# Splitting the down product's operands during the last tiles of the up product, without a fence between the two

## What is computed

```
def conv_ffn(a, buf, w_up, w_conv, b_conv, w_down):
    u = a @ w_up                                   # 1024 -> 2 x 2816
    full = jnp.concatenate([buf, u], axis=1)
    c = b_conv
    for j in range(CONV_W):                        # three taps over time
        c = c + w_conv[j] * full[:, j:j + t]
    gate, val = jnp.split(c, 2, axis=-1)
    y = (jax.nn.gelu(gate) * val) @ w_down         # 2816 -> 1024
    return y, full[:, t:]
```

## Time and profile before

| what | us |
|---|---|
| median of 3 runs | 1949.39 |
| lowest and highest run | 1946.25, 1952.33 |
| the profiled execution's own time | 1946.59 |
| its span, first to last instruction | 1944.8 |
| PE busy in the span | 1807.3 (93%) |
| DVE busy | 1125.4 (58%) |
| ACT busy | 726.3 (37%) |
| PE's part of the chain that ended last | 81% |
| mean granted TensorE clock | 0.959 |

### The profile page before, as it was taken

The page is one execution under the profiler, slowest core; times in us unless marked ns, Lnnn a source line. Parts: engine busy times, 40 slices in busy tenths (PEclk is TensorE's granted clock), DMA queues, the critical chain, the costliest instruction groups (busy, mean ns, idle before and its releaser), DMA issues.

```text
span 1944.8 us, 34321 instructions
## 1 busy us (share of the span) xinstructions
PE 1807.3 (93%) x13384; PEld 1617.6 (83%) x13384; DVE 1125.4 (58%) x2363; ACT 726.3 (37%) x1313; POOL 38.4 (2%) x65
## 2 busy tenths in 40 slices
PE   6899898989999979999999998887989999979997
PEld 5788456989999979988479995445989999979987
DVE  7974465568777652263334865666568777652264
ACT  5323345543233242254323332656543333242252
POOL 1400000000000000000000000000000000000000
PEclk9999788999999989999999996999999999989999
DMA  4133678212222132221031133773212222132211
GB/s 177 66 61 132 212 260 293 87 42 89 87 79 83 41 132 86 78 90 57 21 108 57 55 124 121 265 266 132 88 44 88 87 80 82 41 132 87 77 44 49
DMA packets 77948, 204.13 MB, mean 105 GB/s; under 512 B 12530, under 2 KB 14882, under 8 KB 77314
## 3 DMA queue, kind: packets, MB, share of 16 engines
q1 hardware_dynamic: 75762, 190.36, 29.3%
q0 software_dynamic: 2064, 12.06, 1.8%
HBM read 190.81 MB, written 10.40 MB: 103 GB/s over the span
## 4 chain that ended last, share of the span: by engine, by line
PE 81%; DVE 9%; SPq 3%; ACT 3%; issue 2%; DMA 1%; DVEq 0%; ACTq 0%
PE psum L412 42%; PE psum L585 12%; PE psum L2203 7%; PE psum L2159 4%; PE psum L420 2%; SPq L1312 2%; PE psum L844 1%; PE psum L2352 1%; PE psum L1354 1%; PE psum L507 1%; PE psum L1329 1%; PE psum L521 1%; DVE sb_arena_r L372 1%; DVE sb_ring_r L372 1%; SPq L1296 1%
## 5 line engine op out<-in xcount | busy, mean ns | idle before, releaser
L412 PE MATMUL psum<-sb_a_sb_r,sb_ring_r 128*128 128x288 f32 x1408 | 297.1, 295 | 0.0
L412 PE MATMUL psum<-sb_a_sb_r,sb_arena_r 128*128 128x288 f32 x1344 | 276.5, 296 | 0.0
L412 PE MATMUL psum<-sb_y_sb_r,sb_ring_r 128*128 128x288 f32 x960 | 262.6, 298 | 0.5 <-DVE sb_ring_r L372 0.5
L412 PEld LDWEIGHTS psum<-sb_a_sb_r,sb_ring_r 128*128 128x128 f32 x1408 | 230.9, 188 | 0.4
L412 PEld LDWEIGHTS psum<-sb_a_sb_r,sb_arena_r 128*128 128x128 f32 x1344 | 217.0, 188 | 0.0
L372 DVE TENSOR_TENSOR sb_ring_r<-sb_ring,sb_ring_r 128x1024 fp32r<-128x1024 f32 (+1 forms) x90 | 116.2, 1295 | 169.1 <-ACT sb_ring_r L369 168.1
L412 PE MATMUL psum<-sb_y_sb_r,sb_arena_r 128*128 128x288 f32 x704 | 207.1, 294 | 6.3 <-DVE sb_a_sb_r L372 6.2
L369 ACT ACTIVATE sb_ring_r<-sb_ring 128x1024 fp32r<-128x1024 f32 (+1 forms) x90 | 99.8, 1114 | 300.6 <-PE psum L412 249.3
L412 PEld LDWEIGHTS psum<-sb_y_sb_r,sb_ring_r 128*128 128x128 f32 x960 | 174.9, 189 | 1.6 <-DVE sb_ring_r L372 1.0
L585 PE MATMUL psum<-sb_arena_r 128*128 128x288 f32 x960 | 161.6, 303 | 8.2 <-DVE sb_arena_r L372 8.2
L412 PE MATMUL psum<-sb_arena_r,sb_ring_r 128*128 128x288 f32 x1056 | 146.0, 299 | 20.9 <-DVE sb_arena_r L372 20.9
(11 more groups left out here) (402 smaller groups left out, 3130.2 us busy)
## 6 DMA issues: line engine op xcount, KB each, us to landing
sb_ring<-w SPq DMA_DIRECT2D x166, 512.0 KB, 3.6
sb_ring<-wd SPq DMA_DIRECT2D x32, 704.0 KB, 4.1
sb_arena<-sb_v SPq DMA_DIRECT2D x64, 256.0 KB, 5.5
sb_arena<-moba_v SPq DMA_DIRECT2D x56, 256.0 KB, 6.4
sb_ring<-moba_k SPq DMA_DIRECT2D x32, 256.0 KB, 4.1
sb_a_sb<-moba_k SPq DMA_DIRECT2D x32, 256.0 KB, 5.6
sb_ring<-sb_k SPq DMA_DIRECT2D x32, 256.0 KB, 4.1
sb_a_sb<-sb_k SPq DMA_DIRECT2D x32, 256.0 KB, 5.5
```

The source lines that it names most:

```text
L412: ins = e.eng.matmul(out[:, half, :], fr(w[p][:, k, :]), fr(x[q][:, k, cols]), start=(first and k == 0 and i == 0), stop=(last and k == kb ...
```

## The change

The 22 high parts `ffh` no longer lie in one array. Each block has a place of its own (`ffh_at`): blocks 0 to 3 in free space behind `fo`, blocks 4 to 7 behind the `wx` slabs (where `plew` was), blocks 8 to 14 over the `wx` slabs, blocks 15 to 21 over the convolution's buffers and `fo`. `plew` moves to the place of the first buffers of the convolution. Blocks 0 to 7 thus have places that nothing else uses during the up product.

ACT and DVE split blocks 0 to 7 and down slab 0 between the steps of the last four up tiles. The fence is replaced by a bare `e.mark()` on each engine (the drain and the step on the stage semaphore, with no wait); behind it ACT and DVE go on with blocks 8 to 10 or 12 to 14, slab 1, and the rest. Block 15 and later wait on ACT for the last gated row, blocks 20 and 21 for the store of `fo`, as the last blocks did before. `pe_down` has the same matmuls in the same order, written out because the blocks are now single arrays. SP's queue and POOL's instructions keep their order.

```diff
@@ -1686,6 +1686,7 @@
             tiles(ROUNDS, 2 * REST)
             e.splits += 2 * FT
             acc.skip(2 * FT)
+            e.mark()
 
         def act_up(e, acc):
 
@@ -1702,10 +1703,15 @@
                 act.wait_ge(acc_ready, n0 + n - 3 + i * RING)
                 act_high(e, slabs[:, n % RAW], split[n % 4][0], wh_ready)
 
+            def high_parts(first, last):
+
+                for m in range(first, last):
+                    act.wait_ge(geg_ready, g0 + m + 1)
+                    act_high(e, ff[:, m, :], ffh[m], xh_ready)
+
             def pairs_of(i, count):
                 for j in range(count):
 
-                    pr = 4 * i + j
                     for v in range(2):
                         if not isinstance(i, int) or 8 * i + 2 * j + v + AHEAD < 2 * FT:
                             split_slab(i, 2 * j + v + AHEAD)
@@ -1720,6 +1726,13 @@
                         act.activation(u[:, 2 + TP:TU].rearrange("p (b t) -> p b t", b=NB)[:, :, 2:],
                                        psum[:, 2 * s + 1, TP - HALF:HALF].rearrange("p (b t) -> p b t", b=NB), ACT.Copy)\
                            .then_inc(copied["act"], 1)
+                        if isinstance(i, int) and i == ROUNDS:
+                            if j == 0:
+                                high_parts(3 + 3 * v, (6, 8)[v])
+                            elif v == 0:
+                                act_split_down(e, 0, (acc_ready, n0 + 2 * FT - 2))
+                            else:
+                                high_parts(8, 12)
 
                     act.wait_ge(conv_d, g0 + j + 1 + i * 4)
                     act.activation(cb[2 * (j % 2)], cb[2 * (j % 2)], ACT.Gelu_apprx_tanh).then_inc(conv_a, 1)
@@ -1727,7 +1740,16 @@
             pairs_of(0, 4)
             with act.Fori(1, ROUNDS) as i:
                 pairs_of(i, 4)
+            high_parts(0, 3)
             pairs_of(ROUNDS, REST)
+            e.mark()
+            act_split_down(e, 1, (acc_ready, n0 + 2 * FT))
+            high_parts(12, 15)
+            act.wait_ge(geg_ready, g0 + FT)
+            high_parts(15, 20)
+            act.wait_ge(stored, 16 * (6 if e.downs == 0 else 12))
+            high_parts(20, FT)
+            e.parts += FT
             e.raws = [x + 2 * FT // RAW for x in raws]
             acc.skip(2 * FT)
             e.ups += 1
@@ -1739,6 +1761,17 @@
             base = layer * NVEC
             w0 = e.splits - AHEAD
             v.wait_ge(fst_in, 16 * (layer + 1))
+
+            def low_parts(first, last):
+
+                for m in range(first, last):
+                    v.wait_ge(xh_ready, e.parts + m + 1)
+                    dve_low(e, ff[:, m, :], ffh[m], ff[:, m, :], xl_ready)
+
+            def low_down(n):
+
+                v.wait_ge(wh_ready, w0 + 2 * FT + n + 1)
+                dve_low(e, dslabs[:, n % DRING], *dsplit[n % 2], wl_ready)
 
             def pairs_of(i, count):
                 for j in range(count):
@@ -1769,9 +1802,17 @@
                         o = fo[:, bass.ds(m, 1), :].rearrange("p m x -> p (m x)")
                         v.tensor_copy(o[:, 0:2], u[:, TP:2 + TP])
                         e.st.do(v.tensor_copy(o[:, 2:18].rearrange("p (b j) -> p b j", j=2), us[:, :, TS:TS + 2]))
+                        if isinstance(i, int) and i == ROUNDS and w == 0:
+                            if j == 0:
+                                low_parts(0, 3)
+                            else:
+                                low_down(0)
+                                low_parts(6, 8)
                     v.wait_ge(conv_a, g0 + j + 1 + i * 4)
                     v.tensor_tensor(ff[:, bass.ds(4 * i + j, 1), :].rearrange("p m t -> p (m t)"), cb[2 * (j % 2)],
                                     cb[2 * (j % 2) + 1], ALU.mult).then_inc(geg_ready, 1)
+                    if isinstance(i, int) and i == ROUNDS and j == 0:
+                        low_parts(3, 6)
 
             for u in ub:
                 e.st.do(v.memset(u[:, 0:2], 0.0))
@@ -1780,7 +1821,12 @@
                 pairs_of(i, 4)
                 e.st.leave(ROUNDS)
             pairs_of(ROUNDS, REST)
-            e.splits = w0 + 2 * FT
+            e.mark()
+            low_parts(8, 11)
+            low_down(1)
+            low_parts(11, FT)
+            e.parts += FT
+            e.splits = w0 + 2 * FT + 2
             acc.skip(2 * FT)
             e.ups += 1
 
@@ -1804,7 +1850,13 @@
             ld.end_split(n0 + 2 * FT)
 
 
-        ffh = cut(FT * T, FT * T).rearrange("p (m t) -> p m t", m=FT)
+        PLEW = FT * T
+        late_at = PLEW + 2 * SLAB
+        ffh_at = [18848 + m * T for m in range(4)] + [WX + 4 * SLAB + m * T for m in range(4)] + \
+                 [WX + m * T for m in range(7)] + [late_at + m * T for m in range(7)]
+        ffh = [cut(z, T) for z in ffh_at]
+        assert fo_at + 2 * FT * 18 <= 18848 and 18848 + 4 * T <= WX and WX + 4 * SLAB + 4 * T <= 27952
+        assert late_at + 5 * T <= fo_at < late_at + 7 * T <= 18848 and 7 * T <= 4 * SLAB
 
         def pe_down(e, acc):
             for m in range(KD):
@@ -1813,9 +1865,14 @@
                 for part in range(2):
                     e.splits += 1
                     e.eng.wait_ge(wl_ready, e.splits)
-                    x = [z[:, 11 * part:11 * part + 11, :] for z in (ffh, ff)]
-                    last = mm_split(e, pair(t.s), dsplit[part], x, 11, first=(part == 0), last=(part == 1),
-                                    x_parts=e.parts + 11 * part if m == 0 else None)
+                    for k in range(11):
+                        j = 11 * part + k
+                        if m == 0:
+                            e.eng.wait_ge(xl_ready, e.parts + j + 1)
+                        for half in range(2):
+                            for i, x in enumerate((ffh[j], ff[:, j, :], ffh[j])):
+                                last = e.eng.matmul(pair(t.s)[:, half, :], fr(dsplit[part][i // 2][:, k, :]), fr(x[:, COLS[half]]),
+                                                    start=(j == 0 and i == 0), stop=(j == FT - 1 and i == 2))
                     last.then_inc(part_done if part == 0 else acc_ready, 1)
             e.parts += FT
 
@@ -1827,12 +1884,6 @@
             act_high(e, dslabs[:, slot], dsplit[n % 2][0], wh_ready)
 
         def act_down(e, acc, buf):
-            for n in range(2):
-                act_split_down(e, n)
-            k0 = (fo_at - FT * T) // T
-            act_split_rhs(e, tiles_of(ff, k0), tiles_of(ffh, k0))
-            e.eng.wait_ge(stored, 16 * (6 if e.downs == 0 else 12))
-            act_split_rhs(e, tiles_of(ff, FT)[k0:], tiles_of(ffh, FT)[k0:])
             for m in range(KD):
                 t = acc.next("act")
                 if m < KD - 1:
@@ -1851,9 +1902,6 @@
                 e.eng.wait_ge(wh_ready, e.splits)
                 dve_low(e, dslabs[:, n % DRING], *dsplit[n % 2], wl_ready)
 
-            for n in range(2):
-                low(n)
-            dve_split_rhs(e, tiles_of(ff, FT), tiles_of(ffh, FT), tiles_of(ff, FT))
             for m in range(KD):
                 if m < KD - 1:
                     low(2 * m + 2)
@@ -1865,13 +1913,12 @@
             acc.skip(KD)
 
         yh = cut(0, KD * T).rearrange("p (k t) -> p k t", k=KD)
-        PLEW = 25344
         plew = cut(PLEW, 2 * SLAB).rearrange("p (s k n) -> p s k n", s=2, k=KD)
         hh_, hl_ = (cut(i * KD * T, KD * T).rearrange("p (k t) -> p k t", k=KD) for i in range(2))
         out_sums = [sums(12800), sums(12800 + 3 * T)]
         down_sums = [y_sb[:, 2 * DSLAB + i * T:2 * DSLAB + (i + 1) * T] for i in range(3)]
         gate_sums = [sums(17408), sums(17408 + 3 * T)]
-        assert 17408 + 6 * T <= WX and WX + 4 * SLAB <= PLEW
+        assert 17408 + 6 * T <= WX
 
         def down_tiles(acc):
 
@@ -1882,7 +1929,6 @@
             pe_sweeps(e, acc, out_pairs, (yh, y), out_sums, True)
             e.pre += 1
             pe_up(e, acc, out_sums)
-            e.fence()
             pe_down(e, acc)
 
             t = down_tiles(acc)
```

## The result

| what | before | after |
|---|---|---|
| median of 4 runs beside each other, us | 1949.02 | 1916.86 |
| lowest and highest run | 1946.25, 1952.33 | 1914.17, 1920.96 |
| the profiled execution's own time | 1946.59 | 1917.88 |
| its span | 1944.8 | 1916.1 |
| PE busy in the span | 1807.3 | 1798.6 |

The ratio is 0.9836, with a 95% interval of 0.9812 to 0.986: faster, by 32 us where 23.4 were forecast. Over all runs made in this study, 67 of before and ten of after, the means are 1946.8 and 1917.9, 28.9 us apart. 1916.86 lies 9.1 us under the forecast and 4.6 us under the low end of its range. The sign, the place and, as will be seen, the size at that place were right; the rest of the difference comes from a stage that the change doesn't touch.

What follows compares the result with a forecast made beforehand. PE was taken as the bound, losing about 12.2 us at each of two seams to a pause and slow clock. Savings of 11.73 and 11.62, together 23.4, from the median 1949.39 gave 1926.0 us; range 1921.5 to 1932.0.

Steps and rivals of the forecast that it cites:

- Part 1: Last four up tiles: eight blocks and slab 0 fit DVE's and ACT's idle time at no cost, about 0.3 us spare.
- Part 2: Drain between up and down products: with marks instead of a fence, PE restarts after 0.14 us, at about 681.2.
- the row of 0.14: PE's restart behind the drain, taken from the wait between DVE's last result and PE: 0.14 us.
- Part 3: Middle of first down tile: PE waits 0.4 us for DVE's block 11, until 690.33; then its own 8.74 us cover.
- the sum: Both seams: 11.73 us saved in the first layer, 11.62 in the second, together 23.4.
- The clock: At the seam: granted clock stays at 1.00 from 650 to 720, avoiding the slow first part.
- Case C: Seam: the clock falls anyway and the first part stays slow, 1.5 us per layer, 1929.0 us; chance 0.05.
- case D: ACT's wait for the store: it lands late, costing 5.1 us per layer, 1936 us; chance 0.03.
- Case B: DVE's chain at the seam slips, as by POOL's two issues, 1.2 us per layer, 1928.4 us; chance 0.08.
- All behind it moves along.: Everything after the seams: later stages shift earlier with the seam savings, together 23.4 us.
- the small one of its low end: First down tile: with best PE restart and DVE steps, PE alone sets the middle, 0.5 us a layer more; low end 1921.5.

Runs made afterwards that it cites:

- new places alone: Changed kernel with the fences and old split order back in both layers; only block places and written-out down product stay: 1940.24 us, ratio 0.9959 against before.
- one seam: Changed kernel with the fence and old split order back in the first layer, so the change acts only in the second: 1928.48 us, ratio 0.9906 against before.
- the later start: Changed kernel with 88 extra matmuls ahead of the first layer's first down block: 1938.62 us, ratio 0.9953 against before.
- the third new trace of before: Kernel before, unedited, third of three further single executions: 1937.44 us, recurrence 19.4 us.
- the denser one: Changed kernel with two extra 288-column matmuls in each of the recurrence's four steps: 1920.45 us, ratio 0.986 against before.
- the denser recurrence: Kernel before with two extra 288-column matmuls in each of the recurrence's four steps: 1941.59 us, ratio 0.9984 against before.
- the kernel with the work ahead of the recurrence: Kernel before with two extra 288-column matmuls once, ahead of the recurrence's first step: 1944.04 us, ratio 0.9985 against before.

## Why the prediction was right, and where it was wrong

**Part 1 held.** All three groups fit into DVE's idle time, with 0.38 us to spare ahead of the last convolution (0.3 had been worked out). The convolution of tile 43 starts at 684.63, 0.92 us after PE's last up matmul (0.9), and the product at 687.68, 3.97 after it (3.95). On ACT the four blocks moved the last GELU as worked out, and it cost nothing.

**Part 2 held in its kind, with a small term too low.** PE needs 0.26 us to restart behind the drain, in both layers, where the row of 0.14 was taken and 0.3 was the bound from above.

**Part 3 held.** PE's wait in the middle of the first tile shows as 0.06 instead of 0.4. Of the difference 0.12 is PE's later restart. Most of the rest is a way of counting: 9.00 us run to the end of the 66th matmul, the 8.74 of the prediction from start to start, and neighbouring matmuls overlap. (The next 66 have a row of 8.99 us, and what follows them starts 8.83 behind their start.) Both errors fall into the cover: what sets the middle of the tile is DVE's block 11, counted from the up product's end. That was forecast at 690.33 - 681.05 = 9.28 us and measured at 693.02 - 683.71 = 9.31 and 1693.31 - 1683.99 = 9.32. Against 702.06 - 681.05 = 21.01 before, the first seam gives 11.70 at this point, for 11.73 in the sum, and the second 1722.82 - 1701.92 - 9.32 = 11.58, for 11.62.

**The clock held.** No window between 650 and 720 shows less than 1.00. Case C is out. The kernel with early splits and fences shows how much hung on the short pause: 4.98 us of it and the clock stood at 0.50.

**The stores and POOL.** ACT ran its last ten blocks in one row without a wait, so the store was never late; the stores of `o_ffn` landed in 2.7 to 3.1 us (2.6 before), and case D is out. POOL's two issues took 1.26 us inside DVE's first group behind the product, and that group of three blocks took 2.10 us, where the three blocks at 668.48, with no POOL beside them, took 2.09:

```profile
668.48 2.09 DVE L372 TENSOR_TENSOR sb_arena_r<-sb_arena,sb_arena_r 128x576 fp32r<-128x576 f32 x3
```

Case B is out too. The lock of the port pair that the Trainium skill describes (SBUF — State Buffer, section "SBUF: two separate sides") did not show here: POOL's instructions here only start transfers, while the page's rule is for those that read SBUF. Whether the rule holds for those was not tested.

**A term that was missing inside the seam.** From the end of the up product to the end of the down product there are 140.70 us where 140.3 were forecast. Of the 0.4, 0.33 are in the 990 matmuls behind the middle (131.39 for 131.06), and most of it comes with the new places or the new form of the product: the kernel with the new places and the fences takes 834.58 - 703.28 = 131.30 us for the same 990, 0.24 more than before. The prediction had taken the written-out matmuls, "the same matmuls in the same order", at no cost. What in it costs that, the separate arrays or the longer code, was not tried.

**The step that failed is in the sum: "All behind it moves along."** It takes each later stage to last as long as before. Twice this was not so. The recurrence of the second layer lasted 27.7 us in the execution on which the sum was built and 19.2 in the changed kernel, 8.5 us that no term had; the start of the launch was 2.6 longer. The sum is 23.4; measured were 22.6 by the chains, and 22.3 between two kernels that both showed the short recurrence in their traces (1940.24, the median with the new places and the fences, and 1917.9, the mean of ten runs of the changed kernel). So the 23.4 came true within about 1 us, and the step that failed is that one, not the seam. The range failed with it: it was built from the spread of three runs, all of which were above 1944.4, where most of the 67 lie, and every rival but the small one of its low end made the time longer. (That low end is also 0.4 us off by its own working: 1922.9 less 0.5 a layer is 1921.9.) The page of before gives the granted clock in 40 slices, with a 6 in the 25th; windows over that slice would have shown that PE ran for 30 us at half clock in a stage that the change doesn't touch.

**What is settled of the surplus, and what is not.** Shown is: in the traces the surplus is in the recurrence; there it is the granted clock, at 0.50 in most of the long one and 1.00 in the short one, over the same instructions; it is not the first seam (new places alone, one seam); it is not a fixed start time (new places alone; the later start); and it is not fixed in a kernel (the third new trace of before; the times of the later start, without traces, fit). Three of four traces of before have the long recurrence. Of the eight traces with the new places none has it: six show 19.2 us, the denser one 22.2, the one without fence and with late splits 20.9. The new places and the written-out product alone brought 7 us, clear of the noise, so it is they that shift the odds. Open is how, and which of the two. That the place at which the clock falls is just at the recurrence in before, so that a small shift of what PE does around it decides, is an argument; the denser recurrence fits it, the kernel with the work ahead of the recurrence neither speaks for it nor against it, and for the edits that stand far away it was not shown.

## What to carry to other kernels

A fence between two stages and the placing of the second stage's preparation are one change: each half leaves a pause, and here the halves were worth 12.4 us and the whole 23.3. When a seam is costed, follow the engine that delivers last (DVE's block 11) instead of the one that waits; errors in the waiting engine's own pace vanish in its cover, and the sum was right to 0.03 us there. But before a difference is forecast from one execution, look for stretches at half clock anywhere in it, and compare several executions by stage: one of them was worth 8.5 of 28.7 us here.

## What the runs showed of the hardware

**The granted clock can fall while PE doesn't stand still.** In before it went to 0.50 within the window from 1160 to 1165, in which PE was busy for 5.00 of 5.00 us. PE had last stood still for 1.66 us up to 1155.19 and had then run groups of 128-column, 64-column and 8-column matmuls. It stayed at 0.50 until after 1190, and the recurrence took 27.7 instead of 19.2 us. The same pause of 1.66 us stands ahead of the recurrence in the changed kernel and in the third new trace of before, where the clock held until the last matmuls of the recurrence or beyond; whether it answers to the pause, to the short matmuls or to both is not shown. Two 288-column matmuls more in each of the four steps, which do nothing useful, came with 1.00 through the recurrence in the traced execution.

**Executions of one program differ by this.** 67 runs of before reach from 1935.8 to 1953.4, with the recurrence at 19.4 us in a run of 1937.44 us and at 27.7 in two of 1946; the changed kernel's ten runs reach from 1914.2 to 1921.0. Another part of the spread is elsewhere: the slowest execution of before (1955.35) had a start 5 us longer than the first trace (424.7 against 419.5).

**A drain on PE between two products with nothing to wait for leaves PE idle for 0.26 us**, in both layers; in the kernels with one new seam or the pad it was 0.26 to 0.29. From start to start it is more, as neighbouring matmuls overlap: the last matmul ahead of the drain starts at 683.41, the first behind it at 683.97, 0.56 us later, where one follows another after 0.13.
